# Expert products in plain fp32 column tiles, weights as whole rows, down products one expert late

## What is computed

```python
def ec_moe(h, router, w_up, w_down):
    cap = CAPACITY_FACTOR * T // N_EXPERTS
    aff = jax.nn.softmax((h @ router).astype(jnp.float32), axis=-1)
    gate, idx = lax.top_k(jnp.swapaxes(aff, 1, 2), cap)
    xg = h[bidx, idx]
    up = jnp.einsum('becd,edf->becf', xg, w_up)
    hid = jax.nn.silu(up[..., :D_EXPERT]) * up[..., D_EXPERT:]
    y = jnp.einsum('becf,efd->becd', hid, w_down) * gate[..., None].astype(h.dtype)
    return jnp.zeros_like(h).at[bidx, idx].add(y)
```

## Time and profile before

| | us |
|---|---|
| median of 3 runs | 2186.6 |
| lowest and highest | 2186.19 and 2187.09 |
| span of the profiled execution, first to last instruction | 2185.7 |
| PE busy in it | 1810.2 |
| DVE busy | 1320.3 |
| ACT busy | 996.3 |
| POOL busy | 330.5 |

### The profile page before, as it was taken

The page is one execution under the profiler, slowest core; times in us unless marked ns, Lnnn a source line. Parts: engine busy times, 40 slices in busy tenths (PEclk is TensorE's granted clock), DMA queues, the critical chain, the costliest instruction groups (busy, mean ns, idle before and its releaser), DMA issues.

```text
span 2185.7 us, 24672 instructions
## 1 busy us (share of the span) xinstructions
PE 1810.2 (83%) x8221; PEld 1133.2 (52%) x8221; DVE 1320.3 (60%) x1771; ACT 996.3 (46%) x1141; POOL 330.5 (15%) x268
## 2 busy tenths in 40 slices
PE   4999754938999999999967989989377787878782
PEld 2876221415656565555645766774154545555451
DVE  3641795366756666675514655562677768677771
ACT  4212760134646455554422433551256757566651
POOL 1001344010112111111110322440100101000001
PEclk7999876968999999999988999999688988889896
DMA  9246742177999999999921000001879999999992
GB/s 342 75 147 270 309 155 87 58 271 240 354 352 358 353 354 361 343 362 352 358 76 58 1 0 0 0 0 56 309 251 367 382 368 372 386 357 384 380 323 91
DMA packets 206692, 527.96 MB, mean 242 GB/s; under 512 B 11805, under 2 KB 20138, under 8 KB 200250
## 3 DMA queue, kind: packets, MB, share of 16 engines
q1 hardware_dynamic: 193530, 482.55, 60.2%
q0 software_dynamic: 13120, 44.87, 7.1%
HBM read 504.21 MB, written 23.17 MB: 241 GB/s over the span
## 4 chain that ended last, share of the span: by engine, by line
PE 69%; DVE 10%; ACT 8%; issue 7%; DMA 3%; POOL 1%; SPq 0%; DVEq 0%; ACTq 0%; POOLq 0%
PE duo L718 14%; PE wide L608 6%; PE wide L545 6%; PE wide L686 5%; PE wide L688 5%; PE wide L687 5%; PE turned L458 5%; PE wide L693 4%; ACT sb_w_hi L1050 4%; PE wide L694 4%; PE duo L895 2%; PE wide L872 2%; PE duo L817 2%; DMA sb_ring<-ada_w 1%; PE turned L457 1%
## 5 line engine op out<-in xcount | busy, mean ns | idle before, releaser
L1428 DVE TENSOR_TENSOR sb_w_lo<-sb_ring,sb_w_hi 128x2048 fp32r<-128x2048 f32 x256 | 580.7, 2289 | 128.1 <-ACT sb_w_hi L1050 123.7
L1050 ACT ACTIVATE sb_w_hi<-sb_ring 128x2048 fp32r<-128x2048 f32 x256 | 485.1, 1911 | 324.4 <-PE wide L688 226.4
L718 PE MATMUL duo<-sb_ring_x,sb_hidT 128*96 128x512 f32 (+1 forms) x1024 | 357.2, 627 | 5.3 <-ACT sb_hidT L1075 4.8
L693 PE MATMUL wide<-sb_w_hi,sb_xs 128*128 128x512 f32 x512 | 228.6, 446 | 1.1 <-DVE sb_xs L1440 1.1
L718 PEld LDWEIGHTS duo<-sb_ring_x,sb_hidT 128*96 128x96 f32 (+1 forms) x1024 | 119.4, 157 | 203.1 <-issue 190.6
L694 PE MATMUL wide<-sb_w_lo,sb_xs 128*128 128x512 f32 x512 | 222.0, 434 | 0.0
L686 PE MATMUL wide<-sb_w_hi,sb_xs 128*96 128x512 f32 x512 | 203.8, 398 | 1.7 <-DVE sb_xs L1440 1.7
L688 PE MATMUL wide<-sb_w_hi,sb_xs 128*96 128x512 f32 x512 | 202.5, 395 | 0.0
L687 PE MATMUL wide<-sb_w_lo,sb_xs 128*96 128x512 f32 x512 | 201.4, 393 | 0.0
L1748 POOL DMA_INDIRECT stream<-sb_ye,sb_idx_c x32 | 46.3, 1446 | 852.8 <-DVE sb_ye L1488 427.6
L1436 DVE TENSOR_TENSOR sb_h<-turned,sb_mod_a 128x384 f32<-128x384 f32 (+1 forms) x64 | 31.4, 491 | 210.6 <-PE turned L458 210.6
(11 more groups left out here) (279 smaller groups left out, 2909.4 us busy)
## 6 DMA issues: line engine op xcount, KB each, us to landing
sb_ring<-moe_w_up SPq DMA_DIRECT2D x256, 1024.0 KB, 13.8
sb_ring_x<-moe_w_down SPq DMA_DIRECT2D x128, 1024.0 KB, 6.4
sb_ring<-ada_w SPq DMA_DIRECT2D x48, 1024.0 KB, 8.9
sb_ring<-lru_w_in SPq DMA_DIRECT2D x8, 1024.0 KB, 11.8
sb_ring<-lru_w_out SPq DMA_DIRECT2D x4, 1024.0 KB, 10.8
sb_ring<-mla_w_o SPq DMA_DIRECT2D x4, 1024.0 KB, 6.0
stream<-sb_areaD POOLq DMA_DIRECT2D x6, 512.0 KB, 3.0
normed<-sb_areaC POOLq DMA_DIRECT2D x6, 512.0 KB, 3.8
```

What stands on the lines that cost most here:

```text
L693: mm(o, both, wh[:, k, :], start=first, stop=False)
L718: ins = mm(o, hidT[:, h, kk % 4, 0:M], w[:, k, n * BANK:(n + 1) * BANK], start=kk == 0, stop=kk == KD - 1)
L1050: fn(w_hi[:, j % NW, :], chunk_at(j), ACT.Copy).then_inc(s_hi[lay], 1)
L1428: v.tensor_tensor(w_lo[:, j % NW, :], chunk_at(j), w_hi[:, j % NW, :].bitcast(F32), ALU.subtract).then_inc(used[j], 1)
```

## The change

Both products of an expert become plain fp32, straight from the loaded chunks; `w_hi`, `w_lo`, the split of the rows, and the copies and subtractions are gone. The array's columns are filled with column tiles: the 64 latent rows give pairs (two tiles of 64), the 32 context rows of layer 0 give quads (four tiles of 32), each tile with another block of 512 output columns. A quad of the down product also has two tiles for different halves of the sum, which are added at the end. In layer 0 PE does pairs for two blocks of rows, then quads for the same two blocks, then pairs again.

SP loads an up chunk as 128 whole rows of 2048 numbers (8 KB), and a down chunk as 256 rows, two to a partition (8 KB as well); the hidden rows are therefore transposed with a step of two. The down product of expert i is placed behind the up product of expert i + 1, and rows are gathered two experts ahead. Core of the diff:

```diff
@@ block.sync, experts
+                def load_up(e, n):
+                    for k in range(KD):
+                        sp.wait_ge(used[k], n + USED0[lay][k])
+                        sp.dma_start(chunk_at(k), e[k]).then_inc(landed[k], 16)
+                def load_down(e, n):
+                    for c in range(4):
+                        sp.wait_ge(used[KD + c], n + USED0[lay][KD + c])
+                        sp.dma_start(chunk_at(KD + c), e[c]).then_inc(landed[KD + c], 16)
+                load_up(up[0], 0)
+                load_down(down[0], 0)
+                load_up(up[1], 1)
+                with sp.Fori(0, E - 2) as i:
+                    load_up(up[2:E][i], i + 2)
+                    load_down(down[1:E][i], i + 1)
+                load_down(down[E - 1], E - 1)
...
@@ block.tensor, experts
+                    for group in range(0, KD, 2):
+                        for k in range(group, group + 2):
+                            pe.wait_ge(landed[k], e * 16 + 16 * (LANDED0[lay][k] + 1))
+                            for s in range(2):
+                                for n in range(2):
+                                    at = (2 * s + n) * BANK
+                                    ins = mm(wide[n * CAPL:(n + 1) * CAPL, s, :], xT[:, k, 0:CAPL], chunk_at(k)[:, at:at + BANK],
+                                             start=k == 0, stop=k == KD - 1)
+                            if lay == 1:
+                                ins.then_inc(used[k], 1)
+                        if lay == 0:
+                            for k in range(group, group + 2):
+                                for n in range(4):
+                                    ins = mm(wide[n * CAPC:(n + 1) * CAPC, 2, :], xT[:, k, CAPL:M], chunk_at(k)[:, n * BANK:(n + 1) * BANK],
+                                             start=k == 0, stop=k == KD - 1)
+                                ins.then_inc(used[k], 1)
...
+                turn_rows(0, None)
+                up(0, True)
+                turn_rows(1, None)
+                turn_hid(0, 4)
+                with pe.Fori(0, E - 2) as i:
+                    up(i + 1, False)
+                    turn_rows(i + 2, i + 1)
+                    down(i)
+                    turn_hid(i + 1, i * 2 + 6)
+                up(E - 1, False)
+                down(E - 2)
+                turn_hid(E - 1, 2 * E)
+                down(E - 1)
...
@@ block.scalar, experts
+                def output_rows(e):
+                    act.wait_ge(used[NCH - 1], e + (USED0[lay][NCH - 1] + 1))
+                    act.wait_ge(s_scat[lay], e * 16 + 32)
+                    ins = fn(ye[0:CAPL, BANK:D], duo[CAPL:2 * CAPL, 0, :], ACT.Copy)
+                    if lay == 0:
+                        fn(yc[CAPL:M, 0:BANK], duo[0:CAPC, 1, :], ACT.Copy)
+                        fn(yc[CAPL:M, BANK:D], duo[CAPC:2 * CAPC, 1, :], ACT.Copy)
+                        ins = fn(yd[CAPL:M, :], duo[3 * CAPC:4 * CAPC, 1, :], ACT.Copy)
+                    ins.then_inc(s_yhi[lay], 1)
...
@@ block.gpsimd, experts
                 gather(0)
+                pool.wait_ge(s_xgtr[lay], 2)
+                gather(1)
                 for e in range(E):
                     pool.wait_ge(s_scat[lay], e * 16 + 32)
-                    if e + 1 < E:
-                        pool.wait_ge(s_xgtr[lay], e * 2 + 2)
-                        gather(e + 1)
+                    if e + 2 < E:
+                        pool.wait_ge(s_xgtr[lay], e * 2 + 4)
+                        gather(e + 2)
                     pool.wait_ge(s_ye[lay], e + 2)
```

More of the change, by code:

```diff
@@ L131, in build @@
     USED0, LANDED0 = [None, None], [None, None]
-    NS, NW = 8, 4
     USED0[0] = slot_loads + [1] * (NCH - RING)
@@ L739, in experts, with turn_rows @@
-                body(E - 1, True)
+                MT = M if lay == 0 else P
+                chunk_of = lambda c: chunk_at(KD + c).rearrange("p (r n) -> p r n", r=2)
+                def turn_rows(e, before):
+                    pe.wait_ge(s_gath[lay], e * 16 + 16)
+                    if before is not None:
+                        pe.wait_ge(s_hidT[lay], before)
+                    for part in range(2):
+                        for k in range(4):
+                            ins = turn(turned[:, part, k * MT:(k + 1) * MT], xg[0:MT, (4 * part + k) * P:(4 * part + k + 1) * P])
+                        ins.then_inc(s_xgtr[lay], 1)
@@ L1105, in _ @@
+                silu(0)
+                hidden(0)
+                with act.Fori(0, E - 1) as i:
+                    silu(i + 1)
+                    output_rows(i)
+                    hidden(i + 1)
+                output_rows(E - 1)
             norm_and_logits(0)
@@ L1491, in experts, with rows @@
[L1491 to L1496 removed]
+                steps = 5 if lay == 0 else 3
+                def rows(e):
+                    for part in range(2):
+                        dve.wait_ge(s_xgtr[lay], e * 2 + (part + 1))
+                        k = slice(4 * part, 4 * part + 4)
+                        loop_chain.step(v.tensor_tensor(
+                            xT[:, k, 0:M], turned[:, part, 0:4 * MT].rearrange("p (k m) -> p k m", k=4)[:, :, 0:M], mod_a[:, k, 0:M], ALU.mult))
+                        v.tensor_tensor(xT[:, k, 0:M], xT[:, k, 0:M], mod_b[:, k, 0:M], ALU.add).then_inc(s_xgT[lay], 1)
@@ L1498, in residual_norm @@
+                rows(0)
+                hidden(0)
+                rows(1)
+                dve.wait_ge(s_scat[lay], 32)
+                with dve.Fori(0, E - 2) as i:
+                    loop_chain.n = i * steps + 4
+                    hidden(i + 1)
+                    rows(i + 2)
+                    output_rows(i)
+                loop_chain.n = (E - 2) * steps + 4
+                hidden(E - 1)
+                output_rows(E - 2)
+                output_rows(E - 1)
             def residual_norm(lay):
```

265 lines of the change are left out of this document (76 added, 189 removed).

## The result

The changed kernel takes 2126.6 us (median of four; 2116.9 to 2128.1), the kernel before in the same session 2186.9; the ratio is 0.9715, 95% interval 0.9695 to 0.9736. It is faster, by 60 us. The forecast was 2059, with 2032 to 2108 as its range, so the direction was right and the time was 68 us too low, outside the range.

What follows compares the result with a forecast made beforehand. TensorE bound layer 0; layer 1 was a mixture, close to its loads' limit with TensorE waiting for silu x up. 2185.7 - 47 (layer 0) - 80 (layer 1) = 2058.7, adjusted to 2059.6, rounded 2059 us; range 2032 to 2108.

Steps and rivals of the forecast that it cites:

- TensorE's sums: TensorE, layer 0, per expert: 20.6 + 10.3 + 1.9 + 1.4 + 0.5 = 34.7, taken as 34.8 us, against 37.75.
- third rival: TensorE: each change of tiling costs 0.5 us, 5.6 an expert in layer 0, +90 us, 2149; chance 0.05.
- the fifth: TensorE: 32-row tiles with full 32 columns run one after the other, +30.9 us an expert, 2553; chance 0.03.
- Does anything else hold layer 0?: Layer 0 check of loads, ACT, DVE and POOL's scatter-gather loop; loop taken as about 31 us, hidden behind 34.8.
- Rival 2: Scatter-gather loop sets layer 0: at 36.5 us +25, 2084; at 38.1 us +50, 2109; chance 0.10.
- The ends of layer 0: Layer 0: first expert 26.4 us before the loop; after it 45.8 us through the last down, then 6.9 tail.
- ACT's two copies: Layer 0 after the loop: part of the 45.8 us with up, down, turns and the last down.
- Layer 1: Bound by loads: 2.46 us a chunk, 180 chunks, 2.3 an expert for gather and scatter; 80 us less.
- fourth rival: Layer 1: TensorE's clock stays at 1.2 GHz, an expert takes 45.8 us, +250, 2310, slower than before; chance 0.04.
- the first (395 GB/s): Loads don't gain from whole rows and stay at about 395 GB/s, +35 us, 2094; chance 0.12.
- sixth rival: Gathers and scatters hide between 8 KB packets and all else holds: 34 us less, 2025; chance 0.06.

Runs made afterwards that it cites:

- busy-work experiment: Changed kernel with 16 transposes of the identity, results unused, ahead of each wait for the gather in layer 0: 2112.8 us, ratio 0.9659.
- gather-first kernel: Changed kernel with POOL issuing the gather for expert e+2 before it waits for the last scatter's landing: 2081.1 us, ratio to before 0.9518.

## Why the prediction was right and wrong

**TensorE's sums held.** Up, down, turns and changes in layer 0 were put at 34.8 us, and with the wait gone the experts are 34.6 apart; two and four column tiles overlap fully (3.65 and 1.92 us for 16 records); a change of tiling was taken as 0.12 and measured 0.14 to 0.15. The third rival (0.5 each) and the fifth (quads one after the other) are out. The Trainium skill (TensorEngine Tiling (Array Packing), Key Properties) says that a change of the tiling mode drains TensorE; here such a change cost 0.14 to 0.15 us, which agrees with a short drain. The first product was forecast at 494 us and came at 494.12, in part by luck: the first gather landed after 4.1 us instead of 9.8, but only 1.75 of that is its issue. Before, SP posted loads from 0.2 us ahead of it on; in the changed kernel no load ran beside it, which the prediction does not name.

**The step that failed** is in "Does anything else hold layer 0?": "I take about 31, hidden behind 34.8" for POOL's loop. Its ends had been written down, 27.6, 35.4 and 38.1 us. I took a value near the shortest, because DVE's long two-input operations, which go, seemed to explain the medians of 8.0 and 8.2 us. They explained only the issue (2.74 to 0.95 us). The landings stayed at 9.3 and 8.4, and the loop closed at 36.5. The trace of before could have told it: those medians mix both layers. In the loop of layer 0 (590 to 1000 us) the scatters and then the gathers landed so:

```profile
DMA to landing us min/median/max: 8.2/8.4/8.6
...
DMA to landing us min/median/max: 8.9/8.9/9.0
```

That gives 6.9 + 8.4 + 0.6 + 8.9 + 0.9 + 10.8 = 36.5, or 34.7 with 1.8 us less of issue. Neither is cover for 34.8. What the runs showed in place of the step: the landings are made by the loads in hand. Posting two of them 5.4 us later took 3 us off the scatter's landing and opened the loop. The Trainium skill (DMA: Bandwidth & Descriptors, Queues, rings and completion order) says that a DMA engine takes turns between queues in packets of many descriptors, so that a transfer can wait for a whole packet of another queue. That agrees with a scatter's first packet 5.2 us after its instruction with two loads posted beside it, and 2.0 us after it where no load ran (the last scatter of layer 0); how large a turn is here no run shows. I had written "a packet of 8 KB in front of each 4 KB one", which is too little: at 318 GB/s those 5.2 us are about 12 packets of 8 KB on each of the 16 engines.

Rival 2 was this mechanism, with a chance of 0.10 and a price of 25 to 50 us. The measured price is 45.5. The 36.5 us loop alone gives 1.9 an expert over 34.6; the mean from the first to the fourteenth scatter was 38.2, so 3.6 over it: 2.2 of waiting and 1.3 of slower work behind the waits (6.07 us for a stretch of 3.65), of which the busy-work experiment gave back 0.9. The prediction priced no fall of the clock in layer 0, though it looked for one in layer 1.

**The ends of layer 0** were 12 us dearer than forecast. In the gather-first kernel the first scatter comes 73.1 us after the first product, where the terms give 66.9, and the last two scatters take 53.1 us, where they give 47.0. The second is the wait for expert 14's sums in front of the last down product, 5.28 us, of which my "ACT's two copies" was only a part, and 2.8 us at half clock behind it; the first is likewise half clock at two places and a wait of 4.3 us in front of the transposes of expert 0's hidden rows, where 2.9 was forecast. The hidden rows were ready 2.4 us before it ended; it ended with DVE's modulated rows of expert 1, which the sum had left out. On the other side the loop itself was 0.2 shorter an expert, so that layer 0 without the wait stood 10 us over the forecast.

**Layer 1** went as forecast in kind: bound by its loads, with the split's waits gone, the clock at 0.98 and the DMA engines full to the end. The fourth rival (the clock falls in layer 1) is out, and so is the first (395 GB/s). The size was 12 us off: a chunk takes 2.49 to 2.50 us and not 2.46, which is 6 us on 180 chunks, and rows take 2.5 us an expert and not 2.3, which is 3; the other 3 I have not traced. The sixth rival (rows hide between the packets) is refuted by the run without them. Part of the gain is the row size: 33.0 against 32.55 us with 4 KB rows.

**Sum.** By the table, 58 us of the miss are layer 0, 12 are layer 1, and 4 came back in the stretches between and after: 66.4. The other 1.2 of 67.6 are how the profiled executions stand to their medians, 0.9 before and 2.1 now.

## What to carry to other kernels

When a change shortens the engine that binds, list every loop that runs through another queue and price it by the medians of the stretch in question, not by its best cases, unless the thing that goes is shown to have caused them. A loop of 36.5 us is nothing beside 37.75 of work and is the bound beside 34.6. Waits that guard no data are worth taking out just then: a gather that reads what no scatter writes need not stand behind the scatter's landing.

Where small row transfers share the DMA engines with large loads, look at which loads are posted and not yet moved when the rows are issued; moving a semaphore's increment by one group of products was worth 45 us here.

## What the runs showed of the hardware

With the DMA engines idle at its start, a gather of 96 rows of 4 KB landed after 4.7 us with the loads posted 1.0 us behind it, and after 8.3 with the loads posted 0.3 us behind it. A gather posted right behind a scatter landed after 11.5. Scatters landed after 5.2 to 5.5 us with no load in hand, and after 8.8 with loads in hand that were posted over 6 us before. A change between 64-column and 32-column tiles costs 0.14 to 0.15 us of TensorE. Of 13 waits of 1.8 to 3.3 us in an otherwise full loop, 8 were followed by products at the lower clock (4.78 to 6.15 us for what takes 3.65); waits of 1.84 us are in both groups. 16 transposes of the identity in front of the wait kept the clock at 1.00. Loads with 8 KB rows ran at 421 GB/s over 300 us on this one core.
